# First layer of a two-block model on one core: keys' chunks before the values', a longer preparation table, another order of transfers

## The chip, the core and the metric

The kernel runs on one core of a Trainium2 chip. The engines are TensorE (PE), VectorE (DVE), ScalarE (ACT), GpSimd (POOL) and SyncE (SP), which here issues nearly all transfers. The metric is the device time of one launch in microseconds: 1747.9 us, the median of three runs (1746.54 to 1750.58).

## The reference, cut to what matters

```python
hn = rms_norm(h, pre_norm_g[l]);  proj = hn @ w_in[l]        # 256 tokens, 2048 features
q, kv6, gates, z_a, feat_b, z_b = split(proj)
o_a = nsa_mixer(q, ...)            # sparse part: compressed, chosen and window attention
o_b = rwkv7_mixer(feat_b, ...)     # 16 heads of 64, in two halves of 8 heads
h = h + rms_norm(concat([o_a * silu(z_a), o_b * silu(z_b)]) @ w_out, post_norm_g)

def rwkv7_mixer(feat, ...):
    pf = feat + mu * (prev - feat)                     # "shift", prev is one token earlier
    r, k, v, wd, ad = split(pf)
    w = decay(w0 + tanh(wd) @ w2);  a = sigmoid(a0 + ad @ a2)
    kk = k * k_k;  kk = kk / max(norm(kk per head), 1e-12)
    k = k * (1 + (a - 1) * k_a)
    scan: state = state * w + (state @ -kk) * (kk * a) + v k^T;  y = state @ r
    y = group_norm(y) * ln_w + ln_b + sum(r * k * r_k) * v
```

A second block with two layers follows (differential attention, gated linear attention); the change does not touch it.

## The kernel before, in words

Each weight matrix is multiplied in chunks of 256 columns and each chunk in 4 pieces of 4 row tiles. `Gemm.load` has SP fetch a piece (512 KB) into one of RAW = 6 buffers; ACT rounds it to `w_hi` (L211), DVE makes the rest `w_lo` (L216), and PE multiplies three times for each tile (L244 to L246, or L253 to L255). A load into a buffer waits until DVE has made `w_lo` of the piece 6 earlier. ACT and DVE prepare a piece LEAD = 3 pieces before PE takes it (`side`).

One turn of PE's loop, three products, is called a slot here. The first layer has 992 slots in 32 chunks; a chunk of 256 columns has 32 slots, a piece of it 8. Piece 100 begins at slot 768, and from there each piece 8 slots later.

Everything else of the layer is woven between the slots. `stage_slots` gives a list `at` of slots; at `at[n]` each of PE, ACT and DVE runs its stage n (`pe_stages`, `act_stages`, `dve_stages`). Each engine's order is thus fixed when the kernel is built, and an engine that waits in a stage holds up its next pieces too. For each half `hh` of the heads there is a preparation (`pe_prepare`, `act_prepare`, `dve_prepare`), two groups of the scan (`GROUP_GAPS`), and a finish of four stages. The shift of a quarter of r, k or v is done in pairs of tiles: ACT scales (L1195), DVE adds (L1318). In the preparation ACT forms sigmoids (L1208) and exponentials (L1215 to L1219), then kk (L1226) and its square (L1229); PE sums the squares (L100), ACT takes the root, DVE the reciprocal (L1346), PE spreads it (L995), DVE applies it. POOL forms the gains (L1523), r * r_k (L1528) and two products (L1532, L1535), and at the end of a half adds the bonus (L1539), which raises `half_done`.

`nsa_slots` does the same for the sparse part, from `at[-5]`, the last stage of the second finish. Its first stage waits for `half_done` 2 (PE L484). Then come two compressions (PE L429, which need both 2 MB matrices `cmp_k_w1` and `cmp_v_w1`, loaded by L410), the scores (PE L452), and DVE's copies of the bias tables (L673), which wait for the last of 8 table parts (L2604, L2605: 32 transfers of 24 to 80 KB). DVE's first scaled scores (L629) stand behind these copies, and PE's second scores wait for them. `SparseMixer.loads` gives SP's order: pieces up to `done`, the wait for `half_done` 2 (the arena is in use until then), then matrices, pieces and table parts mixed.

Of the kernel before, what the change touches and what calls it, by code (L numbers as in the profile page):

```python
# [18 lines left out]
ALU = mybir.AluOpType  # L19
# [3 lines left out]
S = 256  # L23
# [344 lines left out]
class SparseMixer:  # L368
# [34 lines left out]
    def loads(self, sp, g, done):  # L403


        k, a = self.k, self.a
        g.load(sp, done)
        sp.wait_ge(k.half_done, 2)
        for n, nm in enumerate(("cmp_k_w1", "cmp_v_w1")):
            sp.dma_start(self.w1[:, n], a[nm][0].rearrange("(l d) o -> d l o", d=P)).then_inc(k.w1_in, 16)  # L410
            g.load(sp, done + 3 + 3 * n)
        sp.dma_start(self.w2[:, 0], a["cmp_k_w2"][0]).then_inc(self.wi, 16)
        sp.dma_start(self.w2[:, 1], a["cmp_v_w2"][0]).then_inc(self.wi, 16)
        sp.wait_ge(k.rows_out, 32)
        parts_a = toeplitz_parts(k, sp, self.bias_a, 0, NSA_A, self.bi)
        parts_b = toeplitz_parts(k, sp, self.bias_b, NSA_A, NSA_H - NSA_A, self.bi)
        for c in range(P // SKEW):
            next(parts_a)
            next(parts_b)
            g.load(sp, done + 7 + c)  # L420
        g.load(sp, g.n)
# [322 lines left out]
def first_chunks(k, w_in, tiles, one_tile, tok):  # L744


    def rows(base, hh):
        return tiles(w_in, C_ZA + (8 + base + 4 * hh) * P, T_FEAT + base + 4 * hh, 2)
    out = [one_tile(w_in, C_ZA + 32 * P, T_RAW_LORA)]
    for hh in range(2):  # L750
        for base in (0, 16, 8):
            out += rows(base, hh)
    out += tiles(w_in, C_KC, T_KC, 2) + tiles(w_in, C_KS, T_KS, 1) + tiles(w_in, C_KW, T_KW, 1)
    out += [one_tile(w_in, C_GATE, T_GATE)]
    out += tok(w_in, C_VS, T_VV, 4, 1) + [chunk("tok", w_in, C_VW, CW, tok(w_in, C_VS, T_VV, 4, 2)[1]["dst"])]
    out += tiles(w_in, 0, T_Q, 4) + tiles(w_in, C_ZA, T_ZA, 4, (k.half_done, 1))
    return out + tiles(w_in, C_ZA + 33 * P, T_ZB, 4, (k.half_done, 2))


def stage_slots(g):  # L760


    def end(c):
        return g.starts[PIECES * (c + 1)] if c + 1 < len(g.chunks) else g.slots
    at = [end(0) + 14, end(0) + 17, end(0) + 22]
    for hh in range(2):
        c = R_RVK + 6 * hh
        now = max(at[-1] + 2, end(c) + 2)
        at.append(now)
        for after, gap in ((end(c + 1), 4), (0, 4), (0, 8), (0, 8), (end(c + 2), 6), (end(c + 3), 4),  # L770
                           (end(c + 4), 4), (end(c + 5), 4), (0, 4), (0, 8), (0, 10), (0, 3), (0, 8), (0, 10), (0, 5)):
# [12 lines left out]


def first_layer(k, a, g, xt, following):


    nc = k.nc
# [13 lines left out]
    weighted = ar[:, 5120:6144].rearrange("p (j t) -> p j t", t=S)  # L803
    rows = k.proj[:, 62:64, :].rearrange("p j t -> p (j t)")
# [95 lines left out]
    with ExitStack() as ctx:  # L900
# [18 lines left out]
        shifted = [(hh, n, u) for hh in range(2) for n in (0, 2, 1) for u in range(4)]  # L919

        def after_shift(hh, n):
            return 2 + shifted.index((hh, n, 3))
# [45 lines left out]
        def pe_prepare(pe, hh):  # L968
# [16 lines left out]
            for _ in range(8):  # L985
                yield
# [3 lines left out]
            mm.then_inc(ss, 1)  # L990
            yield
# [11 lines left out]
            yield  # L1003
            pe.wait_ge(kn, 4 * hh + 4)
# [194 lines left out]
        def act_prepare(act, hh):  # L1199
# [13 lines left out]
            yield  # L1213
            act.wait_ge(ce, hh + 1)
# [4 lines left out]
            nc.scalar.activation(emid[:], mid[:], ACT.Exp, scale=-decay).then_inc(e1, 1)  # L1219
            yield  # L1220
            yield from act_shift(act, hh, 2)
            yield from act_shift(act, hh, 1)
# [7 lines left out]
            yield  # L1230
            act.wait_ge(ss, hh + 1)
            nc.scalar.activation(small, k.ps[0:8, 0, 0:S], ACT.Sqrt).then_inc(nr, 1)
            yield
            yield
            yield
# [88 lines left out]
        def dve_prepare(dve, hh):  # L1324
# [15 lines left out]
            yield from dve_shift(dve, hh, 2)  # L1340
            yield from dve_shift(dve, hh, 1)
# [4 lines left out]
            nc.vector.reciprocal(small, small).then_inc(rn, 1)  # L1346
            yield
            dve.wait_ge(nb, hh + 1)
            nc.vector.tensor_tensor(pair(bt(hh)), pair(bt(hh)), k.ps[:, 0:2, :], ALU.mult).then_inc(kn, 1)
            yield  # L1350
# [15 lines left out]
            nc.vector.tensor_tensor(fac[:], dec[:, :, 0], emid[:, :, 1], ALU.mult).then_inc(x1, 1)  # L1366
            dve.wait_ge(bp, hh + 1)
# [100 lines left out]
        with nc.Block(no_gpsimd_drain=True) as block:  # L1468
            @block.sync
            def _(sp):  # L1470
# [16 lines left out]
                sparse.loads(sp, g, sum(s <= at[-5] + 16 for s in g.starts) + LEAD + 1)  # L1487
# [4 lines left out]
            def _(pool):  # L1492
# [23 lines left out]
                for hh in range(2):  # L1516
# [3 lines left out]
                    pool.wait_ge(f2, after_shift(hh, 2))  # L1520
                    for u in range(4):
                        j = j0 + u
                        nc.gpsimd.tensor_scalar(spare(hh)[:, u, :], aa[:, u, :], k.va[:, A_KA + j:A_KA + j + 1],  # L1523
# [8 lines left out]
                    nc.gpsimd.tensor_tensor(pk, pk, spare(hh), ALU.mult).then_inc(ka, 1)  # L1532
# [1183 lines left out]
```

## Time and profile before

| | |
|---|---|
| median of 3 runs | 1747.9 us (1746.54 to 1750.58) |
| profiled execution | 1748.47 us, its span 1746.6 us |
| PE busy | 1663.0 us, 95% |
| DVE, ACT, POOL busy | 57%, 45%, 6% |
| TensorE clock, mean | 0.976 of full speed |
| end of the first layer's products | about 634 us |

How to read it: PE's busy share shows how much of the span it stands still, and the granted clock how far it runs at the lower of its two levels (1.2 and 2.4 GHz). Idle time of the other engines counts only where PE waits for them.

### The profile page before, as it was taken

What the parts mean: (1) busy time and instruction counts of PE and PEld (TensorE: products, weight loads), DVE (VectorE), ACT (ScalarE), POOL (GpSimd) and SP (SyncE); (2) the same over time, 40 slices, a digit from 0 to 9 for tenths busy, and PEclk for the clock granted to TensorE, in tenths of its full rate; (3) what the DMA queues carried; (4) which work ended last, traced back from release to release, by engine and by line L of the source; (5) the groups of instructions that cost most, each with busy time, mean ns of one, the idle gap of its engine ahead of it and who ended that gap; (6) DMA issues with size and microseconds to landing.
All of it is one profiled execution on the core that took longest, in us unless ns stands there. A gap on an engine that the chain in (4) does not pass through costs nothing. (4 is left out here: it accounts for less than half of the span.)

```text
span 1746.6 us, 32649 instructions
## 1 busy us (share of the span) xinstructions
PE 1663.0 (95%) x14261; PEld 1582.2 (91%) x14261; DVE 996.7 (57%) x1313; ACT 793.7 (45%) x1128; POOL 96.8 (6%) x88
## 2 busy tenths in 40 slices
PE   8999997999997989979999999998998999999899
PEld 7989996999897979979999899998998989999899
DVE  6666646746433743484444578886456664455443
ACT  6542335332333744443433278775445424444432
POOL 2210002100000001040000000000110000000000
PEclk9999999999997999989999999999999999999999
DMA  9643232423194345456666444444553655456362
GB/s 283 188 137 96 88 95 76 131 89 97 38 257 109 108 148 176 139 129 185 179 171 163 128 127 141 146 143 139 191 167 112 204 149 159 143 167 187 126 205 97
DMA packets 253589, 253.79 MB, mean 145 GB/s; under 512 B 9153, under 2 KB 249826, under 8 KB 253192
## 3 DMA queue, kind: packets, MB, share of 16 engines
q1 hardware_dynamic: 252792, 251.50, 49.2%
q8 instruction: 112, 1.84, 0.4%
q0 software_dynamic: 656, 0.21, 0.1%
q14 instruction: 29, 0.24, 0.0%
HBM read 248.99 MB, written 2.69 MB: 144 GB/s over the span
## 5 line engine op out<-in xcount | busy, mean ns | idle before, releaser
L216 DVE TENSOR_TENSOR w_lo<-w_raw,w_hi 128x1024 fp32r<-128x1024 f32 (+1 forms) x452 | 549.1, 1218 | 547.4 <-ACT w_hi L211 546.9
L244 PE MATMUL ps<-xt,w_hi 128*128 128x256 f32 x2736 | 803.4, 294 | 27.0 <-DVE w_lo L216 22.7
L245 PE MATMUL ps<-xt,w_hi 128*128 128x256 f32 x2736 | 780.9, 285 | 0.0
L246 PE MATMUL ps<-xt,w_lo 128*128 128x256 f32 x2736 | 780.1, 285 | 0.0
L211 ACT ACTIVATE w_hi<-w_raw 128x1024 fp32r<-128x1024 f32 (+1 forms) x452 | 470.3, 1045 | 636.7 <-PE ps L246 483.0
L244 PEld LDWEIGHTS ps<-xt,w_hi 128*128 128x128 f32 x2736 | 531.4, 194 | 52.9 <-issue 39.9
L245 PEld LDWEIGHTS ps<-xt,w_hi 128*128 128x128 f32 x2736 | 532.1, 194 | 1.5 <-issue 1.0
L246 PEld LDWEIGHTS ps<-xt,w_lo 128*128 128x128 f32 x2736 | 531.4, 194 | 0.0
L253 PE MATMUL ps<-w_hi,xt 128*128 128x256 f32 x832 | 243.4, 293 | 0.0
L254 PE MATMUL ps<-w_lo,xt 128*128 128x256 f32 x832 | 236.5, 284 | 0.0
L255 PE MATMUL ps<-w_hi,xt 128*128 128x256 f32 x832 | 236.3, 284 | 0.0
L253 PEld LDWEIGHTS ps<-w_hi,xt 128*128 128x128 f32 x832 | 160.5, 193 | 7.6 <-issue 6.1
L254 PEld LDWEIGHTS ps<-w_lo,xt 128*128 128x128 f32 x832 | 160.6, 193 | 0.3
L255 PEld LDWEIGHTS ps<-w_hi,xt 128*128 128x128 f32 x832 | 160.5, 193 | 0.0
L322 DVE TENSOR_TENSOR proj<-ps,rs_bc 128x512 f32<-128x512 f32 (+1 forms) x71 | 48.0, 676 | 46.8 <-PE ps L246 46.5
L1256 ACT ACTIVATE arena<-ps 128x512 f32<-128x512 f32 (+1 forms) x40 | 20.0, 549 | 36.6 <-PE ps L1063 29.2
L1830 ACT ACTIVATE df_sc<-df_sc,df_st 128x128 f32<-128x128 f32 x64 | 28.4, 445 | 7.6 <-DVE df_st L1906 7.6
L1931 DVE RECIPROCAL t_sq<-t_sq 128x256 f32<-128x256 f32 x16 | 27.9, 1744 | 1.0 <-ACT t_sq L1844 1.0
L1429 DVE TENSOR_TENSOR proj<-ps,proj 64x128 f32<-64x128 f32 (+1 forms) x40 | 13.6, 340 | 16.6 <-PE ps L1090 16.0
L1090 PEld LDWEIGHTS ps<-arena 64*64 64x64 f32 x640 | 20.2, 134 | 2.8 <-DVE arena L1415 0.2
L333 ACT ACTIVATE proj<-ps,rs_tok 128x256 f32<-128x256 f32 x18 | 8.5, 470 | 31.3 <-PE ps L255 31.3
L1090 PE MATMUL ps<-arena 64*64 64x32 f32 (+1 forms) x640 | 22.6, 221 | 0.0
(395 smaller groups left out, 1437.5 us busy)
## 6 DMA issues: line engine op xcount, KB each, us to landing
w_raw<-in_a_w_in SPq DMA_DIRECT2D x128, 512.0 KB, 3.7
w_raw<-in_w_in SPq DMA_DIRECT2D x120, 512.0 KB, 3.5
w_raw<-in_b_w_in SPq DMA_DIRECT2D x96, 512.0 KB, 3.7
w_raw<-in_w_out SPq DMA_DIRECT2D x32, 512.0 KB, 3.6
w_raw<-in_a_w_out SPq DMA_DIRECT2D x32, 512.0 KB, 3.3
w_raw<-in_b_w_out SPq DMA_DIRECT2D x32, 512.0 KB, 4.0
arena<-in_x SPq DMA_DIRECT2D x4, 512.0 KB, 6.7
w_raw<-in_w_in SPq DMA_DIRECT2D x8, 256.0 KB, 3.8
```

The costliest lines, as they stand in the source:

```text
L211: k.nc.scalar.activation(k.wh[:, p % RING, :, 0:w], k.raw[:, p % RAW, :, 0:w], ACT.Copy).then_inc(k.hi_made, 1)
L216: k.nc.vector.tensor_tensor(k.wl[:, p % RING, :, 0:w], k.raw[:, p % RAW, :, 0:w], k.wh[:, p % RING, :, 0:w].bitcast(F32), ALU.subtract).th ...
L244: pe.matmul(os, h[:, cs], xt[:, kt, 0:S], start=st and ct == 0, stop=False, skip_group_check=True)
L245: pe.matmul(os, h[:, cs], xt[:, kt, S:2 * S], start=False, stop=False, skip_group_check=True)
L246: last = pe.matmul(os, l[:, cs], xt[:, kt, 0:S], start=False, stop=sp, skip_group_check=True)
L253: pe.matmul(os, xh, h[:, 0:w], start=st and tt == 0, stop=False, skip_group_check=True)
L254: pe.matmul(os, xh, l[:, 0:w], start=False, stop=False, skip_group_check=True)
L255: last = pe.matmul(os, xl, h[:, 0:w], start=False, stop=sp, skip_group_check=True)
L322: k.nc.vector.tensor_tensor(spec["dst"], g.bank(c)[:, 0:nt * S].rearrange("p (j t) -> p j t", j=nt), view(k.rsb[:, 0:1], [[0, nt], [1, S]] ...
L1090: m = pe.matmul(bank(par, 0)[rows_of(q), u * w:(u + 1) * w], diagonal(b[MT], u, q), b[QQ][rows_of(q), u * w:(u + 1) * w], start=True, stop ...
L1830: nc.scalar.activation(sc[:, i % 2, t, rows[tt]], sc[:, i % 2, t, rows[tt]], ACT.Exp, bias=st[:, i % 2, 0, t, tt:tt + 1], accum_out=st[:, ...
L1931: nc.vector.reciprocal(rh, rh).then_inc(l4, 1)
```

## The change

In the first layer's list of chunks the keys' chunks now come before the values' (r, k, v in place of r, v, k), and `shifted` follows. The preparation has 18 stages instead of 16, with other gaps. The keys' shift now lies right behind the exponentials and the values' shift behind the square root. POOL waits for the keys' shift instead of the values', and its gains go to a room of their own, `gains`. With this the stages fall on these slots (worked out from `stage_slots`):

| | before | after |
|---|---|---|
| first preparation, stage 0 to group | 50 to 263 | 50 to 233 |
| second preparation, its first stage | 460 | 430 |
| second: low-rank products (PE) | 468 | 440 |
| second: sum of squares (PE L100) | 514 | 493 |
| second: spreading (PE L995) | 524 | 511 |
| second: transposes (PE) | 545, 550 | 540, 545 |
| second: first group | 555 | 550 |
| `at[-5]` | 750 | 745 |
| sparse: first stage | 766 | 761 |
| sparse: compressions (PE L429) | 821, 832 | 816, 827 |
| sparse: DVE's table copies (L673) | 836 | 831 |
| sparse: second scores (PE L452) | 852 | 847 |

SP now issues 106 pieces ahead of the wait for `half_done` 2 instead of 104, two pieces instead of three behind each matrix, and among the table parts 4 pieces instead of 7.

```diff
 def loads(self, sp, g, done):
-            g.load(sp, done + 3 + 3 * n)
+            g.load(sp, done + 2 + 2 * n)
-            g.load(sp, done + 7 + c)
+            g.load(sp, done + 5 + c // 2)
 def first_chunks(...):
-        for base in (0, 16, 8):
+        for base in (0, 8, 16):
 def stage_slots(g):
-        for after, gap in ((end(c + 1), 4), (0, 4), (0, 8), (0, 8), (end(c + 2), 6), (end(c + 3), 4),
...
+        for after, gap in ((end(c + 1), 4), (0, 6), (0, 12), (0, 8), (end(c + 2), 8), (end(c + 3), 8), (0, 4),
...
 def pe_prepare(pe, hh):
-            for _ in range(8):
+            for _ in range(7):
                 yield
             pe.wait_ge(s2, hh + 1)
...
+            pe.wait_ge(f2, after_shift(hh, 2))
             pe.wait_ge(kn, 4 * hh + 4)
 def act_prepare(act, hh):
             nc.scalar.activation(emid[:], mid[:], ACT.Exp, scale=-decay).then_inc(e1, 1)
-            yield
-            yield from act_shift(act, hh, 2)
-            yield from act_shift(act, hh, 1)
+            keys = act_shift(act, hh, 1)
+            next(keys)
+            yield
+            next(keys)
+            yield
+            yield
             act.wait_ge(f2, after_shift(hh, 1))
...
             nc.scalar.activation(small, k.ps[0:8, 0, 0:S], ACT.Sqrt).then_inc(nr, 1)
+            values = act_shift(act, hh, 2)
+            next(values)
...
+            next(values)
 def dve_prepare(dve, hh):
-            yield from dve_shift(dve, hh, 2)
-            yield from dve_shift(dve, hh, 1)
+            keys = dve_shift(dve, hh, 1)
...
+            values = dve_shift(dve, hh, 2)
+            next(values)                  # behind the reciprocal
...
+            next(values)
+            dve.wait_ge(f2, after_shift(hh, 2))
             dve.wait_ge(bp, hh + 1)
 sync engine:
-                sparse.loads(sp, g, sum(s <= at[-5] + 16 for s in g.starts) + LEAD + 1)
+                sparse.loads(sp, g, sum(s <= at[-5] for s in g.starts) + LEAD + RAW - 1)
 GpSimd:
-                    pool.wait_ge(f2, after_shift(hh, 2))
+                    pool.wait_ge(f2, after_shift(hh, 1))
-                        nc.gpsimd.tensor_scalar(spare(hh)[:, u, :], aa[:, u, :], ...)
+                        nc.gpsimd.tensor_scalar(gains[:, u, :], aa[:, u, :], ...)
```

ACT in the second preparation before, from the exponentials (L1215 to L1219) over the shifts of values and keys (L1195, `arena`) to the square of kk (L1229):

```order
L1215 ACTIVATE proj<-arena 128x1024 [waits rwp_ce]
L1216 ACTIVATE proj<-arena 128x1024
L1218 ACTIVATE proj<-proj 128x1024 [waits rwp_ex]
L1219 ACTIVATE rw_emid<-rw_mid 128x8
L211 ACTIVATE w_hi<-w_raw 128x1024 [waits piece_used,raw_in0]
L1195 ACTIVATE arena<-proj,rw_omu 128x256 [waits half_done,evac_d] x4
L211 ACTIVATE w_hi<-w_raw 128x1024 [waits piece_used,raw_in1]
L1195 ACTIVATE arena<-proj,rw_omu 128x256 [waits evac_d] x4
L211 ACTIVATE w_hi<-w_raw 128x4x128 [waits piece_used,raw_in2]
L1226 ACTIVATE proj<-arena,va 128x256 [waits rwp_f2]
L1226 ACTIVATE proj<-arena,va 128x256 x3
L1229 ACTIVATE proj<-proj 128x1024 [waits rwp_kr]
```

The same place after (the lines are L1222 to L1226, L1201, L1236 and L1239 there):

```order
L1222 ACTIVATE proj<-arena 128x1024 [waits rwp_ce]
L1223 ACTIVATE proj<-arena 128x1024
L1225 ACTIVATE proj<-proj 128x1024 [waits rwp_ex]
L1226 ACTIVATE rw_emid<-rw_mid 128x8
L1201 ACTIVATE arena<-proj,rw_omu 128x256 [waits evac_d] x2
L211 ACTIVATE w_hi<-w_raw 128x1024 [waits piece_used,raw_in4]
L1201 ACTIVATE arena<-proj,rw_omu 128x256 [waits evac_d] x2
L211 ACTIVATE w_hi<-w_raw 128x1024 [waits piece_used,raw_in5]
L1236 ACTIVATE proj<-arena,va 128x256 [waits rwp_f2]
L1236 ACTIVATE proj<-arena,va 128x256 x3
L1239 ACTIVATE proj<-proj 128x1024 [waits rwp_kr]
```

Four scalings of values and one piece less stand between the exponentials and the square.

SP before, from the last pieces ahead of the matrices (L410) to the pieces behind them:

```order
L202 DMA w_raw<-in_w_in 128x4x256 [waits lo_made] x32
L410 DMA arena<-in_cmp_k_w 128x32x128 [waits half_done]
L202 DMA w_raw<-in_w_in 128x4x256 [waits lo_made] x3
L410 DMA arena<-in_cmp_v_w 128x32x128
L202 DMA w_raw<-in_w_in 128x4x256 [waits lo_made] x3
```

And after:

```order
L202 DMA w_raw<-in_w_in 128x4x256 [waits lo_made] x34
L410 DMA arena<-in_cmp_k_w 128x32x128 [waits half_done]
L202 DMA w_raw<-in_w_in 128x4x256 [waits lo_made] x2
L410 DMA arena<-in_cmp_v_w 128x32x128
L202 DMA w_raw<-in_w_in 128x4x256 [waits lo_made] x2
```

Two pieces moved ahead of the wait for `half_done`, and one piece less stands behind each matrix.

## Rows read from the trace of the kernel before

**Rows 1.** The page: busy time; DVE's split of a piece: total us, mean ns.
```profile
PE 1663.0 (95%) x14261; PEld 1582.2 (91%) x14261; DVE 996.7 (57%) x1313; ACT 793.7 (45%) x1128; POOL 96.8 (6%) x88
...
L216 DVE TENSOR_TENSOR w_lo<-w_raw,w_hi 128x1024 fp32r<-128x1024 f32 (+1 forms) x452 | 549.1, 1218 | 547.4 <-ACT w_hi L211 546.9
```

**Rows 2.** Waits of PE, 0 to 650 us: releaser, total us, times, longest us.
```profile
PE ps L244 <- DVE w_lo L216: 12.6, 6, 6.9
...
PE ps L442 <- DVE proj L714: 2.3, 1, 2.3
...
PE ps L995 <- DVE arena L1346: 0.9, 1, 0.9
```

**Rows 3.** Windows of 10 us: busy of PE, PEld, DVE, ACT, POOL; granted clock, DMA.
```profile
110.00:120.00 10.00, 10.00 (x55) 8.56 (x54) 9.90 (x10) 1.06 (x1) 0.00 (x0) 0.83 0.40 114
310.00:320.00 10.00, 10.00 (x55) 8.58 (x54) 8.03 (x9) 2.75 (x4) 0.61 (x1) 0.83 0.18 54
540.00:550.00 10.00, 10.00 (x61) 9.82 (x60) 4.95 (x8) 3.18 (x11) 0.00 (x0) 0.67 0.38 119
550.00:560.00 10.00, 7.71 (x42) 7.06 (x42) 3.72 (x9) 2.07 (x2) 0.00 (x0) 0.67 0.18 54
```

**Rows 4.** PE's timeline: start us, us, then the wait before it.
```profile
103.01 1.89 PE L100 MATMUL ps<-proj,con 128*8 128x256 f32 x8 [0.69 <-ACT proj L1229]
270.99 0.28 PE L244 MATMUL ps<-xt,w_hi 128*128 128x256 f32 x1
271.35 0.28 PE L244 MATMUL ps<-xt,w_hi 128*128 128x256 f32 x1
281.27 0.28 PE L244 MATMUL ps<-xt,w_hi 128*128 128x256 f32 x1
303.58 3.58 PE L100 MATMUL ps<-proj,con 128*8 128x256 f32 x8 [6.76 <-ACT proj L1229]
493.34 0.36 PE L244 MATMUL ps<-xt,w_hi 128*128 128x256 f32 x1 [1.73 <-DVE w_lo L216]
501.97 2.26 PE L429 MATMUL ps<-arena,proj 128*30 128x128 f32 x19 [0.48 <-DMA arena<-in_cmp_v_w]
538.50 0.80 PE L452 MATMUL ps<-proj 128*128 128x128 f32 x2 [7.85 <-DVE arena L629]
```

**Rows 5.** DVE's timeline in the second preparation, and the table wait.
```profile
273.19 2.98 DVE L1318 SCALAR_TENSOR_TENSOR arena<-proj,va,arena 128x255 f32<-128x255 f32 x2
277.83 0.87 DVE L1318 SCALAR_TENSOR_TENSOR arena<-proj,va,arena 128x255 f32<-128x255 f32 x2
535.85 0.19 DVE L673 COPY cbias<-arena 128x35 f32<-128x35 f32 x1 [17.69 <-DMA proj<-bias_rows_dram]
```

**Rows 6.** ACT's timeline: second preparation, then pieces that wait for their transfer.
```profile
293.12 1.04 ACT L211 ACTIVATE w_hi<-w_raw 128x1024 fp32r<-128x1024 f32 x1
300.73 1.70 ACT L1226 ACTIVATE proj<-arena,va 128x256 f32<-128x256 f32 x4 [1.91 <-DVE arena L1318]
...
490.88 1.06 ACT L211 ACTIVATE w_hi<-w_raw 128x1024 fp32r<-128x1024 f32 x1 [9.62 <-DMA w_raw<-in_w_in]
493.92 1.06 ACT L211 ACTIVATE w_hi<-w_raw 128x1024 fp32r<-128x1024 f32 x1 [0.49 <-DMA w_raw<-in_w_in]
503.45 1.06 ACT L211 ACTIVATE w_hi<-w_raw 128x1024 fp32r<-128x1024 f32 x1 [8.47 <-DMA w_raw<-in_w_in]
511.88 1.06 ACT L211 ACTIVATE w_hi<-w_raw 128x1024 fp32r<-128x1024 f32 x1 [3.01 <-DMA w_raw<-in_w_in]
515.85 1.06 ACT L211 ACTIVATE w_hi<-w_raw 128x1024 fp32r<-128x1024 f32 x1 [2.90 <-DMA w_raw<-in_w_in]
```

**Rows 7.** SP's queue around the end of the second half: start us, us.
```profile
440.02 12.22 SPq L202 DMA_DIRECT2D w_raw<-in_w_in  x3
479.35 0.80 SPq L410 DMA_DIRECT2D arena<-in_cmp_k_w  x1
```

**Rows 8.** POOL's timeline: the half's last addition.
```profile
273.36 2.53 POOL L1539 TENSOR_TENSOR proj<-arena,proj 128x1024 f32<-128x1024 f32 x1 [13.33 <-DVE arena L1464]
```

More of the change, by code:

```diff
@@ L769, in stage_slots @@
         at.append(now)
-        for after, gap in ((end(c + 1), 4), (0, 4), (0, 8), (0, 8), (end(c + 2), 6), (end(c + 3), 4),
-                           (end(c + 4), 4), (end(c + 5), 4), (0, 4), (0, 8), (0, 10), (0, 3), (0, 8), (0, 10), (0, 5)):
+        for after, gap in ((end(c + 1), 4), (0, 6), (0, 12), (0, 8), (end(c + 2), 8), (end(c + 3), 8), (0, 4),
+                           (0, 5), (0, 8), (end(c + 4), 5), (0, 5), (0, 8), (0, 4), (end(c + 5), 12), (0, 5), (0, 8),
+                           (0, 5)):
             now = max(now + gap, after + 2)
@@ L803, in first_layer @@
     weighted = ar[:, 5120:6144].rearrange("p (j t) -> p j t", t=S)
+    gains = ar[:, 6144:7168].rearrange("p (j t) -> p j t", t=S)
     rows = k.proj[:, 62:64, :].rearrange("p j t -> p (j t)")
@@ L918, in first_layer @@
         groups = [(hh, ch) for hh in range(2) for ch in range(2)]
-        shifted = [(hh, n, u) for hh in range(2) for n in (0, 2, 1) for u in range(4)]
+        shifted = [(hh, n, u) for hh in range(2) for n in range(3) for u in range(4)]
         def after_shift(hh, n):
@@ L1213, in act_prepare @@
             yield
+            yield
             act.wait_ge(ce, hh + 1)
@@ L1219, in act_prepare @@
             nc.scalar.activation(emid[:], mid[:], ACT.Exp, scale=-decay).then_inc(e1, 1)
+            keys = act_shift(act, hh, 1)
+            next(keys)
             yield
-            yield from act_shift(act, hh, 2)
-            yield from act_shift(act, hh, 1)
+            next(keys)
+            yield
+            yield
             act.wait_ge(f2, after_shift(hh, 1))
@@ L1230, in act_prepare @@
             yield
+            yield
             act.wait_ge(ss, hh + 1)
             nc.scalar.activation(small, k.ps[0:8, 0, 0:S], ACT.Sqrt).then_inc(nr, 1)
+            values = act_shift(act, hh, 2)
+            next(values)
             yield
             yield
+            yield
+            yield
+            next(values)
             yield
@@ L1339, in dve_prepare @@
             yield
-            yield from dve_shift(dve, hh, 2)
-            yield from dve_shift(dve, hh, 1)
+            yield
+            keys = dve_shift(dve, hh, 1)
+            next(keys)
+            yield
+            next(keys)
+            yield
+            yield
+            yield
             yield
@@ L1346, in dve_prepare @@
             nc.vector.reciprocal(small, small).then_inc(rn, 1)
+            values = dve_shift(dve, hh, 2)
+            next(values)
+            yield
             yield
@@ L1366, in dve_prepare @@
             nc.vector.tensor_tensor(fac[:], dec[:, :, 0], emid[:, :, 1], ALU.mult).then_inc(x1, 1)
+            yield
+            next(values)
+            dve.wait_ge(f2, after_shift(hh, 2))
             dve.wait_ge(bp, hh + 1)
@@ L1519, in _ @@
                     pool.wait_ge(sg, 8 * hh + 8)
-                    pool.wait_ge(f2, after_shift(hh, 2))
+                    pool.wait_ge(f2, after_shift(hh, 1))
                     for u in range(4):
                         j = j0 + u
-                        nc.gpsimd.tensor_scalar(spare(hh)[:, u, :], aa[:, u, :], k.va[:, A_KA + j:A_KA + j + 1],
+                        nc.gpsimd.tensor_scalar(gains[:, u, :], aa[:, u, :], k.va[:, A_KA + j:A_KA + j + 1],
                                                 k.omka[:, j:j + 1], ALU.mult, ALU.add).then_inc(ka, 1)
@@ L1531, in _ @@
                     pool.wait_ge(ka, 5 * hh + 4)
-                    nc.gpsimd.tensor_tensor(pk, pk, spare(hh), ALU.mult).then_inc(ka, 1)
+                    nc.gpsimd.tensor_tensor(pk, pk, gains, ALU.mult).then_inc(ka, 1)
                     pool.wait_ge(ka, 5 * hh + 5)
```

## The prediction

> **What bounds the kernel now.** The page first: PE is busy for 1663.0 of 1746.6 us, DVE and ACT for 57% and 45% [rows 1]. PE sets the end, and a change that leaves its work alone can win only where PE stands still or is granted the lower clock. So next the waits of PE up to 650 us, where the first layer lies [rows 2]: 12.6 us for pieces, of which 6.9 us lie at the change of layer, which the edit does not reach, 2.3 us before L442 and 0.9 us before L995. Then PE's timeline for the long ones and their places [rows 4]: 6.76 us for ACT's square L1229 end at 303.58, in the second half's preparation; 1.73, 0.48 and 7.85 us end at 493.34, 501.97 and 538.50, in the sparse part, the last for DVE's L629. The windows show what follows each stall: PE is full, but at a granted clock of 0.67 to 0.83 [rows 3]. So a stall costs twice, once as idle time and once as products at half rate behind it.
>
> The unit of the sum is the slot: at full clock L244 starts again after 0.36 us (270.99, 271.35) [rows 4].
>
> What can be lost or won at the three places, in the profiled execution:
> - First preparation: 0.69 us before the sum of squares [rows 4] and 0.9 before L995 [rows 2] are 1.6 us; the window behind has clock 0.83, so 10 x 0.17 = 1.7 us [rows 3]. Together 3.3.
> - Second preparation: 6.8 us, and some 2.5 us of the waits for pieces just ahead of it (12.6 less 6.9, 1.7 and small ones) [rows 2]; eight sums take 3.58 instead of 1.89 us [rows 4], and the window 310 to 320 loses 1.7 us [rows 3]. Together 9.3 + 3.4 = 12.7.
> - Sparse part: 1.7 + 0.5 + 7.9 + 2.3 = 12.4 us idle [rows 2, 4]; the clock takes 10 x 0.33 = 3.3 us in 540 to 550, 7.7 x 0.33 = 2.5 in the next window [rows 3], and the scores at 538.50 run about 0.7 us longer. Together 12.4 + 6.5 = 18.9.
>
> **The second preparation.** The half starts at 270.99, which is slot 460 before and 430 after. The chain that leads to the exponentials (DVE's shift of r at 273.19 and 277.83 [rows 5], sigmoids, scan, exponentials, behind which ACT takes its next piece at 293.12 [rows 6]) has the same instructions in the same order; they follow each other and not the slots, so its end stays at about 293.1. From there, after: two scalings 0.9, a piece 1.05, two scalings 0.9, a piece 1.05 (a scaling is 1.70 / 4 as in L1226, a piece as at 293.12 [rows 6]) bring ACT to 297.0; DVE has the first pair's shift, a piece of 1.2 us and the second pair's shift of 0.87 us [rows 1, 5] behind that, to about 299.1; then 1.70 us for the scaled keys and 1.05 for their square, as wide as a piece [rows 6]: it is ready at 301.9, and not at 303.5. PE reaches the sum of squares 63 slots after its start, with the low-rank products on the way; they take 3.1 us, for 281.27 is 20 slots behind 270.99 [rows 4]: 10.28 - 20 x 0.36. So 270.99 + 63 x 0.36 + 3.1 = 296.8. It waits 5.1 us, against 9.3 before. The same sum for before (54 slots, 2.5 us lost to the piece) gives 296.0 and a wait of 7.5 where the profile has 6.8, so it is good to a microsecond. Behind that the path is loose up to the transposes, where the values' shift and the bonus now stand last on DVE, behind four products, two more, three pieces and an evacuation: I give this 0.5 us of PE's time (between 0 and 2.6, if DVE's 15 us there face 12.3 us of PE). The clock falls behind a wait of 5 us as behind one of 6.8; one of the two slow stretches may go, 0.9 of 3.4. Sum: 4.2 - 0.5 + 0.9 = 4.6 us gained. Ends: 0 (the chain alone decides) and 12.7.
>
> **The first preparation.** Its chunks space it out: the products of 191 to 228 stand further apart than before. From the keys' last chunk (slot 144) to the sum of squares (163) there are 6.8 us for a piece, two scalings, the shift, four scalings and the square, about 6.7 us by the same rows: just enough. I take 3.0 of the 3.3 us, between 0 and 3.3.
>
> **The sparse part.** Before, SP has issued 104 pieces and then stands from 452 to 479.35 at the wait for `half_done` [rows 7], with the buffers already free for two more. Let T0 be the first matrix's issue (479.35; slot 766 before, 761 after). What each transfer takes is in ACT's waits for pieces [rows 6]: the first matrix with a piece 11.5 us (to 490.88), a piece 1.5 (two of them to 493.92), the second matrix with a piece 9.5 (to 503.45), a table part with a piece 4.0 (511.88 to 515.85), so a part 2.5. Before, ahead of the last table: 11.5 + 2 x 1.5 + 8.0 + 3 x 1.5 + 0.4 for the small weights + 8 x 2.45 + 7 x 1.5 = 57.5; measured 56.5 (DVE goes on at 535.85 [rows 5]). After: 11.5 + 1.5 + 8.0 + 2 x 1.5 + 0.4 + 19.6 + 4 + 2 = 50.0, where the last two terms are the four pieces; less the same 1.0, the tables are there at T0 + 49.0. The wait is cut since two pieces have left the stretch for the idle queue ahead of it and three have gone behind it.
> PE wants its second scores 86 slots behind its first stage, as before. Before it came there at 538.50 - 7.85 = 530.65, T0 + 51.3 [rows 4]. Of this 1.73 us (pieces late behind the first matrix) go: piece 106 lands at T0 + 11.5, and PE needs it at slot 816, T0 + 20. The compressions' 0.48 stay near 0.5 (second matrix at T0 + 21.0, PE at 20.5). So PE is there at T0 + 49.6. From the tables to PE's scores DVE needs the 538.50 - 535.85 = 2.65 us of before (copies, a piece, L629) [rows 4, 5] and an evacuation that now stands between, half as wide as a piece, 0.6: T0 + 52.3. The stall is 2.7 us and not 7.85. The 2.3 us before L442 are DVE's chain against 12 slots, as tight as before: 1.9. Idle: 12.4 - (0.5 + 2.7 + 1.9) = 7.3 gained. Of the 6.5 us at half rate I take 4 as gained, since the wait falls to a third, though 1.6 us of idle time sufficed for a slow window in the first half [rows 2 to 4]. Sum 11.3. Ends: 1.6 (the tables land no earlier) and 18.9.
>
> Total: 4.6 + 3.0 + 11.3 = 18.9 us. The profiled execution took 1748.5 (span 1746.6 and 1.9 around it), 0.6 above the median. 1748.5 - 18.9 = 1729.6, so 1730.
>
> **A rule that speaks against it.** Beside POOL's addition [rows 8] DVE's pair of shifts took 2.98 us, and 0.87 without it [rows 5]. POOL's 13 us of gains and products now start at the keys' shift in both halves and run beside the reciprocal and DVE's products. The Trainium skill (GPSIMD Engine Reference, 1. Specifications) says that GpSimd shares its SBUF interfaces with VectorE, with contention for instructions that have two SBUF inputs. The trace agrees for this pair. If each of POOL's two long products costs DVE the same 2.1 us, and all of it comes to PE, a half loses 4.2 us; then 8.4 of the 18.9 are gone, and the time is 1738. In the second half before, POOL ran beside DVE too, so I count nothing for it.
>
> **Rivals.**
> 1. The second preparation is bound by its chain alone, and its stall moves but does not shrink. For: the chain to 293.1 is unchanged. Against: four scalings and a piece are taken out behind it, and PE comes 9 slots later. 1748.5 - 14.3 = 1734.
> 2. Transfers bind the sparse part: the engines move at the same rate whatever the order, and the tables land as late as before. For: ACT waits 9.6 and 8.5 us for pieces, so transfers and not products set the pace there [rows 6]. Against: 27 us ahead of it in which SP issues nothing [rows 7]. 1748.5 - 4.6 - 3.0 - 1.6 = 1739.
> 3. DVE and POOL hinder each other as above: 1738.
> 4. Slower: table parts go out back to back, with no piece between, and such a stretch of small transfers is slower than the mix. At 2.45 us a part the tables land at T0 + 49; the gain outside this stall is 18.9 - 5.2 = 13.7 us and the stall before was 7.85, so from a stall of 21.5 us the kernel is slower. The stall is 2.7 us plus eight times what a part takes more, so that point is 2.35 us more, 4.8 us a part. At 5.5 us a part the stall is 27 us and the time 1754. For: a part takes longer than its bytes at a piece's rate would. Against: no row shows a part over 2.5 us.
> 5. Nothing measurable: the gains move into new waits, 1747.
>
> **How the numbers follow.** Forecast 0.66, rivals 1 to 5: 0.12, 0.09, 0.05, 0.04 and 0.04. The likeliest case by itself lies between 1721 (the clock recovers wholly and the second stall halves again) and 1738. Two in ten may fall outside; 1719 to 1742 takes in rivals 1 to 3. 0.2% are 3.5 us, what a measurement can tell from no change: faster 0.91, within it 0.05, slower 0.04.
>
> **What would show it.** The wait of PE for the square in the second half falls from 6.8 to about 5 us, and no piece is late ahead of it; the waits at 103 and 109 us are gone; no wait of ACT of 9 us for a piece behind the first matrix; DVE's wait for the tables ends 49 us behind the first matrix's issue; PE's wait before its second scores is under 4 us, and the windows behind have a clock of 0.9 or more. The prediction is wrong if PE waits longer at the transposes of a half, or if the tables take over 55 us.

## The result, and the profile after

The changed kernel took 1731.9 us (median of 4 runs, 1728.5 to 1733.0), the kernel before 1747.2 us beside it (1741.8 to 1750.6): a ratio of 0.9917, with a 95% interval of 0.9895 to 0.9938. The profiled execution took 1728.5 us with a span of 1726.7. The forecast was 1730 us.

That gain lies where the edit is. At the change of layer PE waits as long as before, 6.87 against 6.90 us, but its wait ends 15.8 us earlier. First PE's timeline there in the kernel before, then in the changed kernel (start, duration, and in brackets the wait ahead of it):

```profile
641.16 0.55 PE L244 MATMUL ps<-xt,w_hi 128*128 128x256 f32 x1 [6.90 <-DVE w_lo L216]
```
```profile
625.36 0.55 PE L244 MATMUL ps<-xt,w_hi 128*128 128x256 f32 x1 [6.87 <-DVE w_lo L216]
```

The profiled spans differ by 19.9 us. The 4 us beyond these 15.8 lie in layers that the edit leaves alone and whose longest waits are the same; the runs of one kernel lie as far apart, so they are not counted here.

The waits of PE from 0 to 650 us in the changed kernel (releaser, total us, times, longest) answer to [rows 2]:

```profile
PE ps L244 <- DVE w_lo L216: 7.8, 3, 6.9
PE ps L100 <- ACT proj L1239: 4.6, 1, 4.6
...
PE ps L999 <- DVE arena L1368: 3.2, 2, 2.1
PE ps L452 <- DVE arena L629: 2.0, 1, 2.0
...
PE ps L442 <- DVE proj L714: 0.6, 1, 0.6
PE ps L1170 <- DVE arena L1484: 0.5, 1, 0.5
```

The pieces now cost 7.8 us and not 12.6, of which 6.9 are the change of layer. The square (L1239, before L1229) costs 4.6 instead of 7.5. One line has grown: the spreading of the reciprocal, L999, is L995 of before, and waits 3.2 us instead of 0.9. The 7.9 us at L452 before the second scores are gone; the 2.0 us now under that line are the fourth scores'.

PE's timeline shows the places:

```profile
94.72 2.54 PE L999 MATMUL ps<-arena 8*128 8x256 f32 x8 [2.09 <-DVE arena L1368]
...
291.69 3.58 PE L100 MATMUL ps<-proj,con 128*8 128x256 f32 x8 [4.57 <-ACT proj L1239]
304.04 1.99 PE L999 MATMUL ps<-arena 8*128 8x256 f32 x8 [1.13 <-DVE arena L1368]
...
538.47 1.03 PE L442 MATMUL ps<-con,proj 128*15 128x128 f32 x8 [0.56 <-DVE proj L714]
553.99 0.49 PE L452 MATMUL ps<-proj 128*128 128x128 f32 x2 [1.96 <-DVE arena L629]
```

And the windows at and behind these places, which answer to [rows 3] (busy time of each engine, then the granted clock of PE):

```profile
90.00:100.00 10.00, 7.91 (x43) 6.82 (x43) 9.93 (x9) 2.89 (x4) 1.61 (x1) 0.80 0.60 166
100.00:110.00 10.00, 10.00 (x65) 9.04 (x65) 7.52 (x8) 2.92 (x4) 0.00 (x0) 0.86 0.39 109
...
290.00:300.00 10.00, 8.31 (x40) 5.73 (x41) 3.89 (x4) 5.58 (x8) 9.92 (x10) 0.66 0.23 62
...
530.00:540.00 10.00, 9.44 (x56) 9.17 (x57) 6.76 (x15) 2.86 (x4) 0.00 (x0) 0.68 0.39 107
```

Worked out as the prediction did, idle time plus what the lower clock takes from a full window:
- First preparation: 2.1 idle + 7.9 x 0.20 + 10 x 0.14 = 5.1 us, against 3.3 before. It has lost 1.8 us.
- Second preparation: 4.6 + 1.1 + 0.2 idle + 8.3 x 0.34 = 8.7 us, against 12.7: 4.0 gained. The 12.7 take the clock from the longer sums and one window. From the windows of the kernel before (clock 0.86 and 0.63 in 290 to 310 us, PE busy for 4.3 and 6.4 us) its loss there is 3.0 us in place of 1.7, and the gain is 5.3.
- Sparse part: 0.6 + 2.0 idle + 9.4 x 0.32 = 5.6 us, against 18.9: 13.3 gained.

Together 15.5, which agrees with the medians (15.3) and with the 15.8 us at the change of layer. Two places are in none of these lines. In the second half's finish PE's wait at L1170, L1164 before, falls from 1.60 to 0.52 us. And in two windows of the changed kernel the clock is lower, where the kernel before has 1.00; they lose 9.5 x 0.10 + 10 x 0.07 = 1.6 us:

```profile
460.00:470.00 10.00, 9.48 (x59) 8.08 (x58) 8.27 (x10) 2.51 (x3) 0.00 (x0) 0.90 0.38 105
470.00:480.00 10.00, 10.00 (x80) 10.00 (x79) 5.99 (x9) 3.18 (x3) 2.40 (x1) 0.93 0.54 147
```

The two nearly cancel, so the split is good to about a microsecond for each part, and not better.

What the sparse part owes its gain to stands in two rows of the changed kernel, the first matrix's issue on SP's queue and DVE's first copy out of the finished tables. They answer to [rows 7] and [rows 5]:

```profile
473.24 0.80 SPq L410 DMA_DIRECT2D arena<-in_cmp_k_w  x1
```
```profile
520.42 0.20 DVE L673 COPY cbias<-arena 128x35 f32<-128x35 f32 x1 [12.77 <-DMA proj<-bias_rows_dram]
```

The tables are there 47.2 us behind the first matrix, and 56.5 before.

### Why the reciprocal is late

The new wait is at L999, for the reciprocal L1368. DVE's timeline ahead of it, in the first half of the changed kernel:

```profile
81.17 1.23 DVE L216 TENSOR_TENSOR w_lo<-w_raw,w_hi 128x1024 fp32r<-128x1024 f32 x1 [2.51 <-ACT w_hi L211]
85.19 4.15 DVE L216 TENSOR_TENSOR w_lo<-w_raw,w_hi 128x1024 fp32r<-128x1024 f32 x1 [2.79 <-ACT w_hi L211]
89.26 0.68 DVE L322 TENSOR_TENSOR proj<-ps,rs_bc 128x512 f32<-128x512 f32 x1
89.86 2.83 DVE L216 TENSOR_TENSOR w_lo<-w_raw,w_hi 128x1024 fp32r<-128x1024 f32 x1
92.62 0.27 DVE L1366 TENSOR_SCALAR arena<-arena 8x256 f32<-8x256 f32 x1
92.93 1.74 DVE L1368 RECIPROCAL arena<-arena 8x256 f32<-8x256 f32 x1
```

and POOL's at the same time:

```profile
81.25 4.64 POOL L1555 TENSOR_SCALAR arena<-arena,va 128x256 f32<-128x256 f32 x4
85.87 2.38 POOL L1559 TENSOR_TENSOR arena<-arena 128x1024 f32<-128x1024 f32 x1
88.33 3.27 POOL L1562 TENSOR_TENSOR arena<-arena 128x1024 f32<-128x1024 f32 x1
```

A piece takes 1.23 us beside POOL's scalings (L1555), but 4.15 and 2.83 us beside its two products (L1559, L1562). That is 4.5 us more on a queue behind which the reciprocal stands. Each of the two pieces ends 1.09 us behind the end of one of the products (89.34 against 88.25, 92.69 against 91.60), about the time of a whole piece. ACT's root had been ready at 89.7 us. So the first suspect was the mechanism of the prediction's third rival, to which it gave 0.05; the experiments try it.

### The profile page after: what moved, and what is told of

Read it like the earlier page. It is cut to its first block and busy times, and to the rows that moved or that the text cites. A ratio compares the mean times of both kernels' runs of the same rounds, so it can differ in the third digit from the quotient of the medians.

```text
span 1726.7 us, 32651 instructions
## 1 busy us (share of the span) xinstructions
PE 1657.4 (96%) x14261; PEld 1577.3 (91%) x14261; DVE 999.4 (58%) x1313; ACT 794.2 (46%) x1128; POOL 94.4 (5%) x88
## 5 line engine op out<-in xcount | busy, mean ns | idle before, releaser
L322 DVE TENSOR_TENSOR proj<-ps,rs_bc 128x512 f32<-128x512 f32 (+1 forms) x71 | 48.0, 677 | 52.2 <-PE ps L246 51.9
L1958 DVE RECIPROCAL t_sq<-t_sq 128x256 f32<-128x256 f32 x16 | 27.9, 1747 | 1.0 <-ACT t_sq L1871 1.0
L1456 DVE TENSOR_TENSOR proj<-ps,proj 64x128 f32<-64x128 f32 (+1 forms) x40 | 13.6, 340 | 15.0 <-PE ps L1096 14.3
L1442 DVE TENSOR_TENSOR arena<-ps,con 128x128 f32<-128x128 f32 (+1 forms) x40 | 13.0, 342 | 14.5 <-PE ps L1080 14.3
```

Source lines behind the costliest of these rows:

```text
L322: k.nc.vector.tensor_tensor(spec["dst"], g.bank(c)[:, 0:nt * S].rearrange("p (j t) -> p j t", j=nt), view(k.rsb[:, 0:1], [[0, nt], [1, S]] ...
L1958: nc.vector.reciprocal(rh, rh).then_inc(l4, 1)
```

## The experiments

Ratios are to the kernel before, run beside them on the same chip, with 95% intervals.

### The two parts of the edit by themselves

The sparse part alone, on the kernel before:

```diff
-            g.load(sp, done + 3 + 3 * n)
+            g.load(sp, done + 2 + 2 * n)
...
-            g.load(sp, done + 7 + c)
+            g.load(sp, done + 5 + c // 2)
...
-                sparse.loads(sp, g, sum(s <= at[-5] + 16 for s in g.starts) + LEAD + 1)
+                sparse.loads(sp, g, sum(s <= at[-5] for s in g.starts) + LEAD + RAW - 1)
```

> The kernel before with the edit of the sparse part alone: two pieces more ahead of the wait for half_done, and fewer between the first matrix and the tables. Theory (the three parts of the edit act each by itself): PE loses 12.4 us idle and 6.5 at half rate in this stretch before, and about 2.5 and 3.1 in the changed kernel, so 11 to 13 us are gained here: 1735 us. Tables at T0 + 47 to 49 where before has 56.5; PE's wait before the second scores under 3 us. Rival (the transfers only reach PE in time because the preparation runs differently in the changed kernel): at most 5 us, 1742 or more, with the second scores' wait above 5 us.

Measured: 1733.7 against 1746.9 us, 0.9923 (0.9903 to 0.9944), 13.3 us by the medians. From 480 to 600 us PE has one wait left, where before had four:

```profile
PE ps L442 <- DVE proj L714: 2.7, 1, 2.7
```

The tables are there 46.9 us behind the first matrix (478.89 to 525.83). The preparation has no part in this.

The preparation alone is the changed kernel with those three lines as before:

> The changed kernel with the transfers of the sparse part as before: the preparation alone. Theory (parts add up): second preparation +4.0 us, first -1.8 us (its new wait of 2.1 us at the spreading and the clock behind it), so a gain of 2 to 4 us and 1744 us, and with the sparse part alone it adds up to the whole change. Rival: the preparation holds more of the 15 us than its waits show, 1739 or less, and then the sparse part alone gives under 10.

Measured: 0.9977 (0.9961 to 0.9993), a gain of 4.0 us by the ratio (1.2 to 6.8), 5.8 by the medians. The wait for the square is 4.6, the one at the spreading 3.6 us in all, and the second scores wait 6.8 us, since the tables take 54.8 us (474.33 to 529.16) as the old order of transfers makes them. 13.3 + 4.0 = 17.3 us agrees with the 14.5 us of both together by its ratio (10.8 to 18.3). The parts add up as far as these runs can tell.

### Which pieces hold the tables back

Two pieces more ahead of `half_done`, the rest as before:

```diff
-            g.load(sp, done + 3 + 3 * n)
+            g.load(sp, done + 1 + 3 * n)
...
-            g.load(sp, done + 7 + c)
+            g.load(sp, done + 5 + c)
```

with `done` as in the changed kernel.

> The kernel before with two pieces more ahead of the wait for half_done, and behind it the same piece numbers between the transfers as before. By the prediction's sum 11 pieces instead of 13 lie ahead of the last table, 1.5 us each: tables at T0 + 53.5, PE's wait at the second scores 7.85 - 3 = 4.9 us, the wait of 1.7 us for a piece behind the first matrix gone: 5 to 6 us gained, 1741 to 1742; the rest of the sparse part's gain then comes from the pieces put behind the tables. Rival (the two pieces fill an idle queue and nothing else follows, since the rest is set by the tables' own transfers): tables at T0 + 56, under 2 us gained, 1746.

Measured: 0.9975 (0.9961 to 0.9989), 3.6 us by the medians. The rival had the tables right: 55.8 us (479.04 to 534.81), and PE waits 8.5 us for its second scores, no less than before. The wait of 1.7 us for the piece behind the first matrix [rows 4] is gone, and at the change of layer PE is 1.9 us ahead. The time lies between the two expectations.

The other half: `done` as before, and only `g.load(sp, done + 7 + c // 2)` between the parts.

> The kernel before with three or four of the pieces that stood between the table parts put behind the last table, and nothing more ahead of half_done. Theory from the two runs so far (two pieces more ahead of the wait moved the tables by 0.7 us, the three between the parts by 8.9 us, 3 us a piece): tables at T0 + 47 to 48.5, PE's wait before the second scores 0 to 1 us instead of 7.85, the wait of 1.7 us for a piece behind the first matrix stays; 8 to 10 us gained, 1737 to 1739. Rival (the prediction's 1.5 us a piece, whichever piece it is): tables at T0 + 52, wait 3.4 us, 5 us gained, 1742.

Measured: 0.9957 (0.9942 to 0.9972), 8.0 us by the medians, as expected. The tables come at 50.3 us (479.46 to 529.78), later than expected and earlier than the rival's 52, and the second scores wait 1.4 us.

And the changed kernel with no piece between the parts, `g.load(sp, done + 4)`:

> The changed kernel with no piece at all between the table parts. Theory (3 us a piece, PE already without a wait before its second scores): tables at T0 + 38 to 41 instead of 47.2, and no more than 1 us gained or lost, 1730 to 1733. Rival (pieces are then late): a wait of PE for a piece of 2 us or more behind T0 + 40, 1735. Rival 4 of the prediction (parts back to back are slow, over 4 us each): tables later than T0 + 50 and a new wait before the second scores, 1740 or more.

Measured: 1732.6 us, 0.9917 (0.9895 to 0.9938), the same as the changed kernel. DVE copies the tables at 516.03, 42.2 us behind the first matrix (473.80), without a wait, so they were there by then. PE could not use them: it had no wait before its second scores any more. Table parts back to back are thus not slow, and the fourth rival falls.

The pieces issued between the first matrix and the last part, and when DVE copies the tables (us behind the first matrix):

| kernel | pieces | tables |
|---|---|---|
| before | 13 | 56.5 |
| preparation alone | 13 | 54.8 |
| two ahead | 11 | 55.8 |
| fewer between | 10 | 50.3 |
| sparse part alone | 8 | 46.9 |
| changed kernel | 8 | 47.2 |
| products behind the reciprocal (below) | 8 | 49.3 |
| none between | 4 | 42.2 at most |

From 13 to 4 pieces it is 14.3 us at least, 1.6 us a piece, about the prediction's price. A single step is not so even, and its price depends on the other. Two pieces less ahead of the parts bring 0.7 us while a piece stands between all parts, and 3.4 us (50.3 to 46.9) once three of those are gone. Three less between the parts bring 6.2 us without the two ahead and 8.9 us with them. Each figure is from one trace, and kernels with the same order of transfers differ by up to 2.4 us here, so the 0.7 us is not told from nothing. Why it is uneven was not settled. SP's timeline bears on it. An issue among the parts takes 0.43 us as a rule. In the kernel with two ahead six of them take 1.3 to 2.2 us, as this one does, and in the kernel before six take 1.0 to 2.3 us. In the sparse part alone there is one, of 1.45 us:

```profile
503.00 2.21 SPq L2604 DMA_DIRECT2D arena<-bias_rows_dram  x1
```

So SP's queue is held up among the parts when a piece stands between all of them, and what two pieces less had won ahead of the parts is used up there. With two ahead the first part goes out 19.1 us behind the first matrix where the kernel before has 22.2, but the last issue of the parts comes 46.5 us behind it where it has 47.1.

### POOL's products beside DVE

In the changed kernel, POOL's two products start behind DVE's reciprocal:

```diff
                     pool.wait_ge(ka, 5 * hh + 4)
+                    pool.wait_ge(rn, 2 * hh + 2)
                     nc.gpsimd.tensor_tensor(pk, pk, gains, ALU.mult).then_inc(ka, 1)
```

> The changed kernel with POOL's two long products (gains times keys, weighted times keys) put behind DVE's reciprocal. Theory (these products slow DVE, pieces of 4.15 and 2.83 us instead of 1.22, and by that make the reciprocal late): DVE's pieces there take 1.2 to 1.3 us again, the reciprocal is done at about 92 us where the changed kernel has 94.6, PE's wait at the spreading is gone in both halves (2.1 and 1.1 us) and the clock behind it in the first; 3 to 6 us gained, 1726 to 1729. Rival (the 13 slots between the square root and the spreading are too few for table load, root and reciprocal whatever POOL does): the wait of 2 us stays, 1732. Second rival (the slowing moves to DVE's four products, which then are late for the transposes): a new wait there of 1 to 3 us, 1731 to 1734.

Measured: 1730.0 us, 0.9895 (0.9877 to 0.9913). DVE's timeline of this kernel, over the same rows as above:

```profile
85.18 1.35 DVE L216 TENSOR_TENSOR w_lo<-w_raw,w_hi 128x1024 fp32r<-128x1024 f32 x1 [2.79 <-ACT w_hi L211]
86.91 0.69 DVE L322 TENSOR_TENSOR proj<-ps,rs_bc 128x512 f32<-128x512 f32 x1 [0.38 <-PE ps L246]
88.06 1.22 DVE L216 TENSOR_TENSOR w_lo<-w_raw,w_hi 128x1024 fp32r<-128x1024 f32 x1 [0.46 <-ACT w_hi L211]
89.75 0.28 DVE L1366 TENSOR_SCALAR arena<-arena 8x256 f32<-8x256 f32 x1 [0.46 <-ACT arena L1243]
90.06 1.74 DVE L1368 RECIPROCAL arena<-arena 8x256 f32<-8x256 f32 x1
```

The pieces take 1.35 and 1.22 us, the reciprocal starts 2.9 us earlier, the wait at L999 is gone in both halves, and the clock is 1.00 from 90 to 110 us. Second rival: also true in part, with 1.1 and 1.3 us of new waits at the transposes (L1018). In net, PE is 3.4 us ahead at the second half's sum of squares (288.26 against 291.69) and the first matrix goes out 2.5 us earlier (470.75 against 473.24). Behind it this is lost again: the tables are copied at 520.08, all but the 520.42 of the changed kernel, and PE waits 1.9 us before the second scores and 1.3 us for the second matrix, where the changed kernel has neither above 0.2. The medians differ by 2 us and the intervals of the ratios overlap: the mechanism is shown, a shorter time of this kernel is not.

If it is the transfers that took the gain back, fewer pieces between the parts should give it back. Both edits together, products behind the reciprocal and `done + 4`:

> POOL's two long products behind the reciprocal, and no piece between the table parts. Theory (the products' move gained 3.4 us up to the second half and 2.5 up to half_done, and the stretch behind it, where transfers set the pace, gave it back as waits of 1.9 us before the second scores and 1.3 us for the second matrix): the 1.9 us go and the gain shows, 1727 to 1729. Rival (what was lost behind T0 is the clock's scatter between runs, not the tables): 1730, as with the products moved alone.

Measured: 1727.7 us, 0.9894 (0.9872 to 0.9915). The copy of the tables comes 42.4 us behind the first matrix (471.07 to 513.51) and the wait before the second scores is gone, though 1.7 us at L442 and 1.5 at L435 take part of its place. By the median it is in the expected range; the ratio's interval does not tell it from the kernel without this edit. The traces do point that way: PE's wait at the change of layer ends at 623.5 us here, at 626.3 with the products moved alone and at 625.4 in the changed kernel.

The opposite cure leaves POOL as it is and lets PE come later, at slot 199 instead of 191, in the first half alone:

```diff
-                           (0, 5), (0, 8), (end(c + 4), 5), (0, 5), (0, 8), (0, 4), (end(c + 5), 12), (0, 5), (0, 8),
-                           (0, 5)):
+                           (0, 5), (0, 8), (end(c + 4), 5), (0, 5), (0, 16 - 8 * hh), (0, 4), (end(c + 5), 7 + 5 * hh),
+                           (0, 5), (0, 8), (0, 5)):
```

> The changed kernel with PE's spreading of the reciprocal 8 slots later in the first half alone (slot 199 instead of 191), POOL's products as they are. Theory (the slowed pieces make the reciprocal late by about 3 us, and PE would reach slot 199 2.9 us later): DVE's pieces there still take 3 to 4 us, but the wait of 2.1 us at the spreading in the first half is under 0.3, and the clock of 0.80 behind it rises: 2 to 4 us gained, 1728 to 1730, as much as moving the products gave up to the second half. Rival (the spreading is no limit of its own; DVE's four products behind it are, and PE waits at the transposes instead): a new wait of 1 us or more before L1018 in the first half, 1732.

Measured: 1727.4 us, 0.9889 (0.9873 to 0.9905). DVE's pieces still take 4.18 and 2.83 us, as predicted, but PE has no wait at L999 in the first half and none at its transposes. The interval overlaps that of the changed kernel, so a shorter time is not shown. The windows behind:

```profile
90.00:100.00 10.00, 10.00 (x68) 9.35 (x67) 9.93 (x10) 3.04 (x3) 0.69 (x1) 0.88 0.63 194
100.00:110.00 10.00, 10.00 (x72) 9.04 (x72) 9.86 (x13) 3.98 (x6) 0.00 (x0) 0.95 0.36 113
```

So what made PE wait in the first half was the meeting of a late reciprocal with 13 slots of room; either side alone mends it. The clock is another matter: with no wait at all it still takes 10 x 0.12 + 10 x 0.05 = 1.7 us here, so of the 3.0 us in the changed kernel only about 1.3 went with the stall. Elsewhere the waits differ by under 1 us (1.5 us at L442 for 0.6, 1.4 at the second half's L999 for 1.1).

### More room for the second half

In the changed kernel, the second half's sum of squares 9 slots later and 4 of them taken back before the bonus:

```diff
-                           (0, 5), (0, 8), (end(c + 4), 5), (0, 5), (0, 8), (0, 4), (end(c + 5), 12), (0, 5), (0, 8),
-                           (0, 5)):
+                           (0, 5), (0, 8 + 9 * hh), (end(c + 4), 5), (0, 5), (0, 8), (0, 4), (end(c + 5), 12 - 4 * hh),
+                           (0, 5), (0, 8), (0, 5)):
```

> The changed kernel with the second half's sum of squares 9 slots later, 5 slots in all, and nothing else: POOL's products and the table parts as in the changed kernel. Theory (the wait is chain against slots): the wait of 4.6 us at the square falls to 1.3 us, the sums take less than 3.6; the wait at the spreading stays at 1.1 or grows to 2 with POOL's products beside DVE; 3 to 5 us gained, 1727 to 1729. Rival (PE's wait only moves to the spreading, 13 slots behind, since DVE and POOL hinder each other there): a wait of 3 us or more at L999, 1731 to 1732.

Measured: 1735.7 us, 0.9936 (0.9921 to 0.9951): no gain, by the medians 4 us more than the changed kernel, though the intervals of the ratios overlap. The rival holds in its mechanism. The wait for the square fell to 1.34 us as both said, but at L999 PE now stands for 4.66 us and runs on the lower clock behind it. PE's timeline and window:

```profile
304.19 3.78 PE L999 MATMUL ps<-arena 8*128 8x256 f32 x8 [4.66 <-DVE arena L1368]
```
```profile
300.00:310.00 10.00, 5.81 (x18) 4.59 (x19) 7.36 (x8) 0.00 (x0) 2.21 (x1) 0.61 0.35 107
```

DVE's and POOL's timelines say why:

```profile
297.19 2.83 DVE L216 TENSOR_TENSOR w_lo<-w_raw,w_hi 128x512 fp32r<-128x512 f32 x1 [1.71 <-ACT w_hi L211]
299.94 2.42 DVE L1366 TENSOR_SCALAR arena<-arena 8x256 f32<-8x256 f32 x1
302.40 1.74 DVE L1368 RECIPROCAL arena<-arena 8x256 f32<-8x256 f32 x1
```
```profile
297.07 2.40 POOL L1559 TENSOR_TENSOR arena<-arena 128x1024 f32<-128x1024 f32 x1
299.54 2.67 POOL L1562 TENSOR_TENSOR arena<-arena 128x1024 f32<-128x1024 f32 x1
```

POOL's products hang on DVE's shift of the keys and not on PE: that shift ends POOL's wait (its first gain starts at 288.31 here and at 289.02 in the changed kernel), and POOL then works up to its products without a pause. Putting PE's sum later therefore put the reciprocal's step right beside POOL's products: half a piece takes 2.83 us, and the maximum over 8 x 256 elements, 0.28 us elsewhere, takes 2.42.

The same room with the products out of the way, no piece between the parts, and 3 slots more before the transposes of each half:

```diff
+                    pool.wait_ge(rn, 2 * hh + 2)
...
-            g.load(sp, done + 5 + c // 2)
+            g.load(sp, done + 4)
...
-                           (0, 5), (0, 8), (end(c + 4), 5), (0, 5), (0, 8), (0, 4), (end(c + 5), 12), (0, 5), (0, 8),
-                           (0, 5)):
+                           (0, 5), (0, 8 + 9 * hh), (end(c + 4), 5), (0, 5), (0, 8), (0, 4), (end(c + 5), 12 - 4 * hh),
+                           (0, 5), (0, 11), (0, 5)):
```

> As pool_none, with the second half's sum of squares 9 slots later behind its stage and the transposes of both halves 3 slots later. Theory (PE's 4.6 us wait at the square is the chain against slots; 12 slots more, 4.3 us, take it to about 0.3): that wait under 1 us, the eight sums at 1.9 us instead of 3.6, clock 1.0 in 290 to 300, waits at the transposes 2.4 us less; 5 to 8 us gained over pool_none, 1720 to 1723. Rival (half_done now comes 11 slots later and the wait moves into the sparse part or the end of the layer): 1727 to 1729.

Measured: 1722.2 us (1717.7 to 1724.0), 0.9859 (0.9836 to 0.9882), the fastest of all, and its interval lies below that of the changed kernel. There is no wait for the square nor at L999, and 1.0 us at the second half's transposes; where the kernel before stood for 6.8 us and the changed one for 4.6, the windows read:

```profile
280.00:290.00 10.00, 10.00 (x85) 10.00 (x85) 8.09 (x11) 8.40 (x14) 0.57 (x1) 1.00 0.35 87
290.00:300.00 10.00, 10.00 (x77) 8.68 (x76) 5.49 (x7) 6.61 (x12) 7.06 (x9) 1.00 0.60 182
300.00:310.00 10.00, 10.00 (x58) 8.87 (x58) 9.90 (x9) 3.34 (x6) 5.40 (x2) 0.83 0.33 102
```

By the medians, room that cost 4 us by itself comes here with 5 us less than the kernel with the other two edits (1727.7). Both pairs of intervals overlap, and the 3 slots before the transposes came with it, so what each of these edits gives is not shown; shown is that all of them together beat the changed kernel.

## Why the prediction was right, and where it was not

The time is 1.9 us from the forecast. The sum was 18.9 us and the trace has 15.5: the terms are off by -0.6, -4.8 and +2.0 us, so part of the agreement is luck: errors that cancel.

- **Second preparation**, 4.6 us forecast, 4.0 measured. The chain was read rightly: the wait for the square is 4.57 us where 5.1 was worked out. Its absolute times are all about 10 us late (the square is ready at 291.6 and not at 301.9), since slot 430 comes at about 261 us and not at 270.99; this drops out of the wait. What was wrong is the path behind it. The prediction called it loose up to the transposes and gave 0.5 us there; the transposes wait 0.2 us, the spreading 1.1. The cause is that of the first half: the maximum L1366, 0.28 us elsewhere, takes 2.48 us there and ends 0.15 us behind POOL's second product (299.73 + 2.48, 298.79 + 3.27).
- **First preparation**, 3.0 us gained forecast, 1.8 us lost. The wait for the square did go, so the term worked out for that chain held. The failed step is "I count nothing for it", the decision on POOL's products. Its reason was that POOL had run beside DVE in the second half before too. It had, and there the maximum took 0.67 us. In the first half the larger price was in the trace of before, read as something else: the 0.9 us before L995 [rows 2] were put down to the spacing of the slots, while DVE's timeline in that place (kernel before) shows the same maximum at eight times its length, ending with POOL's product:

```profile
105.62 2.18 DVE L1344 TENSOR_SCALAR arena<-arena 8x256 f32<-8x256 f32 x1 [0.24 <-ACT arena L1232]
```
```profile
104.39 3.27 POOL L1535 TENSOR_TENSOR arena<-arena 128x1024 f32<-128x1024 f32 x1
```

  The third rival's size was right: 2.1 us a product, 4.2 a half, and the two pieces in the first half are 4.5 us longer. Of these, 2.1 us reached PE as idle time, and the clock behind it took 3.0 us where it took 1.7 before. Moving the products, and giving PE 8 slots more, each removed the wait: the cause of the wait is shown. That of the clock's whole loss is not, since 1.7 us of it stayed without a wait.
- **Sparse part**, 11.3 us forecast, 13.3 measured, and 13.3 with that part alone. The tables were forecast 49.0 us behind the first matrix and came at 47.2; the stall before the second scores was to be 2.7 us and is none, and L442 waits 0.6 and not 1.9. A stall of 2.0 us at the fourth scores, which no term had, stands in their place. The clock gave back 3.5 of 6.5 us, for 4 taken; the window 530 to 540 has 0.68, where the prediction asked for 0.9 or more. Wrong in detail is the share of the causes: two pieces ahead were to bring 3 us and three behind 4.5, and by the runs the two bring 0.7 alone or 3.4 behind the others, and the three 6 to 9. The five together brought 9.3 us, 1.9 a piece where 1.5 were counted; that one price for every piece came so near is luck.
- **Rivals.** Chain alone (1734): falls, the stall shrank from 6.8 to 4.6 us. Transfers bind the sparse part (1739): falls for the edit as made. But its mechanism probably limits what a better preparation can bring, since the kernel with the products moved lost its 2.5 us in this stretch; the medians alone do not show it. Slow parts (1754): falls with none between. Nothing measurable (1747): falls, the ratio's interval ends at 0.9938.

On the rule that spoke against the change: DVE's pieces beside POOL's two products took 2.8 to 4.2 us for 1.2, and the piece beside POOL's scalings 1.23. The Trainium skill (GPSIMD Engine Reference, 1. Specifications) names VectorE instructions in a 2-port perf mode or with two SBUF inputs as those that contend; the trace agrees for the pieces, which have two. The 8 x 256 maximum has one input and is held up too; in which mode it runs no row here shows. The Trainium skill (SBUF — State Buffer, Who interferes with whom) says that the shared port pair is an exclusive lock; the rows agree, for the maximum ends 0.14 and 0.15 us behind POOL's product in the two kernels shown above (107.80 and 107.66 before, 302.36 and 302.21 in the kernel with more room alone).

## What to carry to other kernels

When an edit moves one engine's long instructions beside another's queue, look in the old trace for the same pair and compare each instruction's duration with its usual one; a short instruction at eight times its length is a price, even if PE hardly waits. Room given to one stage is worth only what stands next on the chain, so check what will run beside it at the new time, and move both together. When a gain upstream vanishes, look for a transfer that lands at the same absolute time in both runs, as the tables did here (520.08 and 520.42).

## What the runs showed of the hardware

- A DVE instruction that meets one of POOL's two-input products is not slowed by a share but stands until that product is done: a maximum of 0.28 us became 2.42 and ended 0.15 us behind the product, and pieces of 1.22 us became 4.15 and 2.83 and each ended 1.09 us behind one. DVE's evacuation out of PSUM (L322, 0.68 us at 89.26) ran at its usual length in the middle of such a product, and so did a piece beside POOL's scalings.
- It goes both ways. With the products behind the reciprocal, POOL's first product took 3.88 us instead of 2.38, beside DVE's pieces.
- The granted clock did not fall only behind long stalls: between 28 and 247 us the kernel with the later spreading has no wait of PE in its timeline, and still shows 0.88 and 0.95 in the two windows above. In the changed kernel it fell from 528 us on, ahead of the wait of 0.56 us that ends at 538.47, and PE's last wait had ended at 465.99:

```profile
528.00:530.00 2.00, 2.00 (x19) 2.00 (x18) 1.99 (x2) 0.00 (x0) 0.00 (x0) 0.88 0.47 163
530.00:532.00 2.00, 2.00 (x10) 2.00 (x11) 1.75 (x4) 0.00 (x0) 0.00 (x0) 0.50 0.87 229
```
